# Six of the gate block's matmuls moved between the small score matmuls of compressed attention (two-block network, one core)

## The reference, cut to what matters

```python
sc = jnp.einsum('bghqd,bgnd->bghqn', q_raw, k_cmp)      # 8 heads, 512 queries, 31 compressed keys, depth 64
p_c = masked_softmax(sc, cmp_end[None, :] <= t[:, None])
o_c = jnp.einsum('bghqn,bgnd->bghqd', p_c, v_cmp)
...
gate_a, gate_b = jnp.split(jax.nn.sigmoid(g_merge), 2, axis=-1)   # g_merge: a slice of h @ w_in
merged = gate_a * (o_a @ w_up_nsa) + gate_b * (o_b @ w_up_gla)
```

## Time and profile before

| | before |
|---|---|
| runs | 1431.15, 1431.47, 1431.84 us; median 1431.47 |
| span of the profiled execution, first to last instruction | 1429.1 us |
| the median less the span | 2.4 us |
| PE busy | 1414.6 us (99%) |
| DVE, ACT, POOL busy | 797.8, 538.7, 171.8 us |
| mean granted clock of PE | 0.998 |

### The profile page before, as it was taken

How to read it: one execution, slowest core, us unless ns; L and a number is a source line. 1 busy time by engine, 2 the same in 40 slices (tenths; PEclk the granted TensorE clock), 3 DMA queues, 4 the chain that set the end, 5 groups by cost and what they waited for, 6 DMA issues and landing times.

```text
span 1429.1 us, 17649 instructions
## 1 busy us (share of the span) xinstructions
PE 1414.6 (99%) x7315; PEld 1150.5 (81%) x7315; DVE 797.8 (56%) x1123; ACT 538.7 (38%) x767; POOL 171.8 (12%) x145
## 2 busy tenths in 40 slices
PE   7999999999999999999999999999999999999998
PEld 6888788988888888887888776668888888888887
DVE  6998674744234343367494577774545545434433
ACT  6232334643233132255543337662343223212214
POOL 1030013100000000120141612111210000000002
PEclk9999999999999999999999999999999999999999
DMA  7322224112322322323244211112322232232221
GB/s 200 112 89 89 89 89 147 60 60 89 118 89 89 115 92 89 104 89 97 87 89 119 72 60 60 31 31 60 118 89 89 90 116 89 90 116 89 89 88 60
DMA packets 134879, 129.90 MB, mean 91 GB/s; under 512 B 14688, under 2 KB 130288, under 8 KB 134768
## 3 DMA queue, kind: packets, MB, share of 16 engines
q1 hardware_dynamic: 133664, 125.11, 27.9%
q0 software_dynamic: 992, 3.47, 0.8%
q10 hardware_dynamic: 144, 0.20, 0.0%
HBM read 126.27 MB, written 2.10 MB: 90 GB/s over the span
## 4 chain that ended last, share of the span: by engine, by line
PE 97%; DVE 1%; ACT 1%; issue 1%; DMA 0%; ACTq 0%
PE gemm L461 75%; PE gemm L569 3%; PE gemm L946 2%; PE misc L967 2%; PE misc L986 1%; PE misc L795 1%; PE gemm L653 1%; PE misc L600 1%; PE gemm L730 1%; PE gemm L600 1%; PE gemm L1027 1%; PE gemm L959 1%; PE misc L959 1%; PE gemm L1060 1%; PE gemm L674 1%
## 5 line engine op out<-in xcount | busy, mean ns | idle before, releaser
L1661 DVE TENSOR_TENSOR w_lo<-w_raw,w_hi 128x2048 fp32r<-128x2048 f32 (+1 forms) x108 | 246.7, 2284 | 174.9 <-ACT w_hi L1123 174.8
L461 PE MATMUL gemm<-h_hi,w_hi 128*128 128x512 f32 x828 | 325.2, 393 | 0.0
L461 PE MATMUL gemm<-h_hi,w_lo 128*128 128x512 f32 x828 | 322.5, 390 | 0.0
L461 PE MATMUL gemm<-h_lo,w_hi 128*128 128x512 f32 x828 | 322.5, 389 | 0.0
L1123 ACT ACTIVATE w_hi<-w_raw 128x2048 fp32r<-128x2048 f32 (+1 forms) x113 | 213.8, 1892 | 143.6 <-PE gemm L461 139.5
L461 PEld LDWEIGHTS gemm<-h_hi,w_hi 128*128 128x128 f32 x828 | 155.5, 188 | 35.3 <-issue 2.4
L461 PEld LDWEIGHTS gemm<-h_hi,w_lo 128*128 128x128 f32 x828 | 155.5, 188 | 32.4
L461 PEld LDWEIGHTS gemm<-h_lo,w_hi 128*128 128x128 f32 x828 | 155.5, 188 | 32.2 <-issue 0.5
L461 PE MATMUL gemm<-n_hi,w_hi 128*128 128x512 f32 x336 | 131.0, 390 | 0.0
L461 PE MATMUL gemm<-n_lo,w_hi 128*128 128x512 f32 x336 | 130.8, 389 | 0.0
L461 PE MATMUL gemm<-n_hi,w_lo 128*128 128x512 f32 x336 | 130.8, 389 | 0.0
(11 more groups left out here) (464 smaller groups left out, 1977.6 us busy)
## 6 DMA issues: line engine op xcount, KB each, us to landing
w_raw<-in_w_in SPq DMA_DIRECT2D x62, 512.0 KB, 4.6
w_raw<-in_w_down SPq DMA_DIRECT2D x32, 512.0 KB, 4.0
w_raw<-in_w_up SPq DMA_DIRECT2D x28, 512.0 KB, 4.3
w_raw<-in_w_ffn_gate SPq DMA_DIRECT2D x22, 512.0 KB, 4.5
w_raw<-in_w_ffn_up SPq DMA_DIRECT2D x22, 512.0 KB, 4.4
w_raw<-in_w_ffn_down SPq DMA_DIRECT2D x16, 512.0 KB, 4.0
w_raw<-in_w_o SPq DMA_DIRECT2D x8, 512.0 KB, 4.0
w_raw<-in_w_out SPq DMA_DIRECT2D x8, 512.0 KB, 4.3
```

Source lines behind the costliest of these rows:

```text
L461: mm = nc.tensor.matmul(bank[:], w(s)[:, kt, col0:col0 + P], x(n), start=first, stop=last)
L1661: V.tensor_tensor(part(lo_of(s), s), part(raw_of(s), s), f(part(hi_of(s), s)), SUB).then_inc(S("lo_done"), SLABS_AT[s])
```

## The change

Behind the eight score matmuls of each of the first three query tiles, two matmuls of gate block 6 are issued (numbers 12 and 13, 14 and 15, 16 and 17), and behind the last tile the remaining six (18 to 23) where there were twelve. Nothing is added or left out on any engine, no wait is added, and no other engine's order is changed.

```diff
                     if t == TT - 1 and q == 3:
                         mm.then_inc(S("cmp_scores"), 1)
-        gate_part(6, 12, 24)
+            if t < TT - 1:
+                gate_part(6, 12 + 2 * t, 14 + 2 * t)
+        gate_part(6, 18, 24)
         gate_block(7)
         pe.wait_ge(S("cmp_scaled"), 2)
```

## The result

| | before | changed |
|---|---|---|
| runs, median | 1431.79 us (21 runs) | 1433.78 us (21 runs) |
| lowest and highest | 1430.27, 1433.71 | 1431.63, 1439.63 |
| span of the profiled execution | 1429.1 | 1430.9 |
| mean granted clock of PE there | 0.998 | 0.997 |

The changed kernel is slower, by a ratio of 1.0016 (95% interval 1.001 to 1.0021); the medians differ by 2.0 us. A second set (11 runs of the changed kernel, 33 of the kernel before) gave 1434.13 against 1431.44 us (ratio 1.0019, 1.001 to 1.0028). The shift is inside 0.2%, and these numbers of runs tell it from no change all the same.

A forecast was written before the change was run, and what follows sets the result against it. PE was taken to bound the kernel, with DVE only 1.43 us behind the scores to spare. A renewed clock fall costs 0.97 to 1.7 us, halfway 1.3: 1431.47 + 1.3 = 1432.8 us, range 1431.1 to 1434.0.

The forecast's parts named there:

- The gain of 1.56 us by keeping the clock: Eight gate matmul distances behind the scores take 3.38 us at half clock, 1.82 at full; at most 1.56 us to win.
- The price of a break, 0.32 us: Switching between small and gate matmuls costs PE 0.32 us at each of three breaks, 0.97 us in all.
- DVE moves by the whole 2.33, and the gain becomes a wait for the low part: Scores end 2.33 us later, DVE's softmax and low part too; PE waits and starts the next slab 1.02 us later.
- What is given back at `scores(1)`, 0.31: ACT no longer holds up `scores(1)`, so its distance behind `scores(0)` shrinks from 0.73 to 0.42 us, winning 0.31.
- the case in which the clock holds: Rival, chance 0.28: full clock around the scores, the wait for DVE eats the gain; 0.7 us later, 1432.2 us.
- The clock falls again: 0.97 to 1.7 later: Fall in the last part of the mix or behind it; end 0.97 to 1.7 us later, chance 0.45.
- the forecast's case: The clock falls again in or behind the mix and DVE's delay decides; 1.3 us later, 1432.8 us, chance 0.45.
- if it falls at 837.6 as now: The last 1.3 us of the mix are slowed, taken as 1.0 us; the end comes 1.7 us later.
- Thinner by records: The mix has 12 records per us against 15 before the old fall, so a fall is likelier than not.
- Free switching: Rival, chance 0.12: switching costs nothing in so short a break; scores 1.36 us later, end 0.26 earlier, 1431.2 us.
- The second fall behind the idle time: Rival, chance 0.15: PE idles before transposes and next slab, the clock falls behind; 2.3 us later, 1433.8, up to 1434.6.

The follow-up runs named there:

- low part early: Changed kernel with ScalarE's high part and VectorE's low part of the first merge_a slab ahead of the softmax; median 1431.36 us, ratio 1.0008 to before.
- Four in each break: Changed kernel with four gate matmuls in each of the three breaks and none behind the last tile; median 1433.78 us, ratio 1.0018 to before.
- One in each break: Changed kernel with one gate matmul in each of the three breaks and nine behind the last tile; median 1434.31 us, ratio 1.0021 to before.
- One break of six matmuls: Changed kernel with the six gate matmuls in one break behind the second tile; median 1431.46 us, ratio 0.9995 to before.
- six ahead: Kernel before with the same six gate matmuls ahead of all small score matmuls, no break; median 1431.82 us, ratio 1.0002 to before.

## Why the prediction came out as it did

*The gain of 1.56 us by keeping the clock.* The size of what a fall costs stood: the one near 651 us costs 1.6. In one of the two profiles of the changed kernel the clock did hold.

*The price of a break, 0.32 us.* Right: three breaks cost 0.96 (17.91 against 16.95), and the distances of the starts are those of the rows. The rule of the Trainium skill (TensorE: Matmul & The Clock Gate, section "Packing small matmuls"), by which a weight load overlaps running matmuls only where the row groups differ, was used in the prediction; the runs agree with it: 0.34 and 0.33 at each break of two, against 0.227 inside a run of gate matmuls.

*DVE moves by the whole 2.33, and the gain becomes a wait for the low part.* Right. From the first mask matmul to the end of the low part it was 846.04 - 832.55 = 13.49 before and 849.70 - 833.85 = 15.85 after, 2.36 more. (One step of the working is off: with the transposes at 846.5 the next slab could start at 846.5 + 0.79 = 847.29, not at 846.88. Nothing hangs on it, as the low part comes later.) Experiment "low part early" removed the wait and 0.9 us.

*What is given back at `scores(1)`, 0.31.* Its size was 0.40 (0.73 to 0.33). Hence the case in which the clock holds costs 0.52 and not 0.71.

*The clock falls again: 0.97 to 1.7 later.* This is the term that was mis-sized: 2.5 measured, for 1.7 at most in the forecast's case. The place was right: "if it falls at 837.6 as now", 4.5 us behind the first small matmul; it was 4.4. The slowed rest of the mix cost 1.20 (the last small pair lies 7.56 behind the mask matmul in one profile of the changed kernel and 6.36 in the other), where I took 1.0. But I let the clock rise again after 3.4 us, as in the trace of before, and then only 0.5 us are lost on the gate matmuls behind the mix. It was low for 6.8 us. From 842.07 to 846.02 nine distances took 3.95 us where full clock takes 0.34 + 8 x 0.227 = 2.16: 1.8 lost. PE is then the last again, not DVE, and the interval is 2.5 longer instead of 1.7. PE's own sum gives it: 0.97 for the breaks, 1.20 and 1.8 for the low clock, less the 1.56 of the old fall, 2.4.

*The forecast and the chances.* 1432.8 was the middle of a case that costs 2.5; the medians of the two sets were 2.0 and 2.7 above before. The two kinds of execution cost 0.5 and 2.5 in the interval, and falls elsewhere (1.6 near 651 us in both profiles of the changed kernel) add to some runs of either kernel. So the median depends on how often each kind comes, which I had no row for; that 1433.78 lies inside my range owes much to the range's width. The ratio stays within 0.2%, but I called this bound what a measurement can tell, and 0.16% was told apart from nothing.

*Thinner by records.* I held a fall likelier than not because the mix has 12 records per us against 15. That measure does not sort the kernels. Four in each break has 76 records in 7.2 us, 10.5 per us, and no mean clock below 0.998. One in each break has 51 records in the 4.3 us ahead of its fall, 11.8 per us, and no mean clock above 0.997.

*The rivals.* The clock held in part of the executions, for 0.5. Free switching is refuted. The second fall behind the idle time was not seen: the first profile has PE idle for 1.16 us ahead of line 948 and full clock behind it. The rule of the Trainium skill (TensorE: Matmul & The Clock Gate, "Why this matters for your kernels") that idle gaps bring the clock down does not describe the falls near the scores: PE was busy in all of the stretch ahead of each. The fall at 23.1 us in "low part early" did have PE idle around it.

*Open.* Why one execution falls and the next does not: the same instructions gave both in the changed kernel. Where the falls of the single runs lie, since only the profiled ones have a trace. Why the early low part made low clocks rarer. And whether the wait for GpSimd, which lengthened one run to 1438.93 us, also lengthened the four runs of the kernel before near 1439 us and four more of others above 1437; why that one operation took 5.47 us is open too.

## What to carry to other kernels

Before work is mixed into a stretch to keep the clock up, work out when the mixed stretch ends and who waits for that; here DVE had 1.4 us to spare and the mix used 2.3. One break of six matmuls was better than three of two (fewer switches, and higher mean clocks), though not shown faster than none. A thin mix can do worse than none: where small matmuls ran behind a fall, the clock stayed down twice as long.

When single events of 1.5 us decide, measure the changed stretch by itself, from a fixed matmul ahead of it to one behind, and look at the mean clock of every run before two spans are compared. And read the trace of the slowest run from its start: in the one at hand the 6.5 us lay in the first 32.

## What the hardware showed unexpectedly

Inside the program every fall of the clock in the profiles lasted 3.4 or 6.8 us, and none anything between. The same 64 small matmuls ran with a fall behind them (before) and without (six ahead). At the low level of 1.2 GHz the small matmuls slow down nearly as much as the large: 16 records in 1.85 us for 1.01, gate matmuls 0.427 apart for 0.227. And an elementwise operation of DVE on 16 columns once took 1.20 us for 0.17 while GpSimd wrote 128x512 tiles. One operation of GpSimd on a 128x256 tile took 5.47 us in one execution.
